# The modulation vectors of a two-block model on one Trainium2 core: where their 96 slabs of weights are multiplied, and by which engine

## The chip, the cores and the metric

The program runs on one core of a Trainium2 chip. The metric is device time in microseconds (us) from start to end of one execution, the lower the better; the time stated for a kernel is the median of several executions.

The engines are called TensorE (PE in the profile, with PEld for its weight loads), VectorE (DVE), ScalarE (ACT), GpSimd (POOL) and SyncE (SP, which here only starts transfers). Each runs its own list of instructions in order, and waits on semaphores for the others.

## The reference, cut to what matters

The model is one block (delta rule, dilated attention, expert layer) and then two layers of a second block, over 512 latent tokens and 256 context tokens of width 1024. The change touches only the six modulation vectors of each layer of the second block:

```
s_lat = jax.nn.silu(c)
s_ctx = jax.nn.silu(c_ctx)
for i in range(DEPTH_2):
    mod = (s_lat @ w_mod[i] + b_mod[i])[:, None, :]
    mod_c = s_ctx @ w_mod[i] + b_mod[i]
    sh1, sc1, g1, sh2, sc2, g2 = jnp.split(mod, 6, axis=-1)
    ...
    h = rms_norm(x, norm_mix[i]) * (1.0 + sc1) + sh1
    ...
    x = x + g1 * y
    h = rms_norm(x, norm_ffn[i]) * (1.0 + sc2) + sh2
    x = x + g2 * swiglu(h, w_gate[i], w_up[i], w_down[i])
```

`w_mod[i]` is 1024 x 6144 in fp32. Two vectors (latent and context) are multiplied with it, so there are 6144 x 2 results a layer: much to load (24 MB a layer) and little to compute. Nothing in it depends on the tokens, so it may be done at any time before its first use.

## The kernel before

**Slabs.** All weights come as slabs of 128 x 1024 fp32 (512 KB), in one list called `spine`, through four buffers `raw0` to `raw3` that `load_sync` fills in the order of the list. Slab i may be loaded when slab i-4 is done with its buffer.

**Units.** A slab of an ordinary weight is a *unit*: ScalarE rounds it to `whi` (L524), VectorE subtracts to get `wlo` (L532), each into one of three buffers, and TensorE does 24 matmuls: 16 with `whi` (L600, L602) and then 8 with `wlo` (L611). The buffer `raw` is free when `wlo` is made.

**Modulation.** `w_mod` is 96 slabs: six groups (l, r), l the layer and r the third of its 6144 columns, of 8 row blocks k times 2 halves. In `mod_tensor` a slab is two fp32 matmuls with a stationary operand of 32 columns (`svec`, the two input vectors) and 512 columns of the slab streamed; half 0 uses columns 0 to 63 of the array, and half 1 columns 64 to 127. The halves of one k stand next to each other in the list and run as one *pair* of slabs, four column groups side by side, in one PSUM bank a group. When a group's 16 slabs are done, `mod_end` copies the bank to SBUF on ScalarE, transposes it on TensorE (L932) and adds the bias on VectorE (L942, L949).

**Order.** Everything is laid out before the kernel is built by a planner (`Weave`): it keeps a clock for each engine, with costs for each kind of instruction, and each side stream (an attention lane, a chain) places its next step when its inputs are expected. `split_ahead` places the splits of up to two units ahead of the one that runs. `drain` runs side streams alone, when no unit may go on. The stages, by the trace's time: the convolutions' units (to about 100 us), delta rule and dilated attention beside projections `u_da` (to 527), four units of the merge and `u_z` (to 588), 20 units of the merge and `u_out` (to 764), the context's two layers and the experts, and then each latent layer: its mixer's units and local ("near") attention, output projection, feed-forward network (`net0`, `net1`).

**Where the slabs stand before.** `coupled(main, halves)` spreads pairs over a list of units: 8 pairs beside the convolutions, 8 beside the last 12 units of `u_da`, 16 beside 26 units of the merge and `u_out`, 1 + 13 beside `net0`, and 2 at the start of the second latent layer. (The first pairs of these last two stand just ahead of the first units of their stage.) In the near attentions there is nothing of them: `lat` calls `drain` for the four lanes, of which each item does scores, softmax, eight transposes (L2562), and the product with the values (L2571), on pairs of PSUM banks listed in `near_lane`.

## Time and profile before

| | |
|---|---|
| time, three runs | 3846.35, 3853.12, 3858.47 us; median 3853.12 |
| span of the profiled execution | 3848.4 us (it has no other time of its own) |
| TensorE busy | 3718.6 us, 97% of the span |
| VectorE busy | 2396.7 us, 62% |
| ScalarE busy | 1577.5 us, 41% |
| GpSimd busy | 840.9 us, 22% |
| memory traffic | 647 MB, 168 GB/s over the span |

### The profile page before, as it was taken

What the parts mean: (1) busy time and instruction counts of PE and PEld (TensorE: products, weight loads), DVE (VectorE), ACT (ScalarE), POOL (GpSimd) and SP (SyncE); (2) the same over time, 40 slices, a digit from 0 to 9 for tenths busy, and PEclk for the clock granted to TensorE, in tenths of its full rate; (3) what the DMA queues carried; (4) which work ended last, traced back from release to release, by engine and by line L of the source; (5) the groups of instructions that cost most, each with busy time, mean ns of one, the idle gap of its engine ahead of it and who ended that gap; (6) DMA issues with size and microseconds to landing.
All of it is one profiled execution on the core that took longest, in us unless ns stands there. A gap on an engine that the chain in (4) does not pass through costs nothing.

```text
span 3848.4 us, 56344 instructions
## 1 busy us (share of the span) xinstructions
PE 3718.6 (97%) x22665; PEld 3215.4 (84%) x22665; DVE 2396.7 (62%) x4154; ACT 1577.5 (41%) x2538; POOL 840.9 (22%) x695
## 2 busy tenths in 40 slices
PE   8999999989999999999999999998999999899998
PEld 5788777788899899999999999777777777677887
DVE  6455433466899668888888887567533345764333
ACT  4523343444335653333333335446422243653222
POOL 0112000153116454344344343010100010100000
PEclk9999999999999999999999999999999999899999
DMA  5211245533355679999999995320333432112332
GB/s 206 82 47 45 91 141 184 194 108 100 96 175 190 221 253 358 345 330 346 325 345 332 346 333 184 94 76 28 111 121 126 137 131 69 58 39 88 99 95 75
DMA packets 213908, 647.03 MB, mean 168 GB/s; under 512 B 19760, under 2 KB 65840, under 8 KB 210064
## 3 DMA queue, kind: packets, MB, share of 16 engines
q1 hardware_dynamic: 162816, 459.47, 35.8%
q0 software_dynamic: 50832, 183.95, 13.1%
q8 instruction: 180, 2.95, 0.3%
q14 instruction: 80, 0.66, 0.1%
HBM read 615.13 MB, written 27.79 MB: 167 GB/s over the span
## 4 chain that ended last, share of the span: by engine, by line
PE 86%; DVE 8%; ACT 4%; issue 1%; DMA 1%; POOL 0%; SPq 0%; DVEq 0%; ACTq 0%
PE ps L600 22%; PE ps L611 22%; PE ps L602 21%; PE ps L557 4%; PE ps L3502 2%; PE ps L2544 1%; PE ps L2571 1%; PE ps L2562 1%; PE ps L909 1%; DVE hlo_plain L774 1%; ACT l_NS L2594 1%; PE ps L2147 1%; PE ps L1240 1%; PE ps L1575 1%; PE ps L1231 1%
## 5 line engine op out<-in xcount | busy, mean ns | idle before, releaser
L600 PE MATMUL ps<-hhi,whi 128*128 128x512 f32 (+1 forms) x2824 | 1060.5, 376 | 3.6 <-DVE xres L3089 2.9
L532 DVE TENSOR_TENSOR wlo<-raw,whi 128x1024 fp32r<-128x1024 f32 x543 | 666.6, 1228 | 598.7 <-ACT whi L524 588.9
L602 PE MATMUL ps<-hlo,whi 128*128 128x512 f32 (+1 forms) x2824 | 1033.1, 366 | 0.2
L524 ACT ACTIVATE whi<-raw 128x1024 fp32r<-128x1024 f32 x616 | 648.5, 1054 | 596.9 <-PE ps L611 410.2
L611 PE MATMUL ps<-hhi,wlo 128*128 128x512 f32 (+1 forms) x2824 | 653.7, 370 | 0.0
L600 PEld LDWEIGHTS ps<-hhi,whi 128*128 128x128 f32 x2824 | 532.7, 189 | 104.1 <-issue 23.5
L602 PEld LDWEIGHTS ps<-hlo,whi 128*128 128x128 f32 x2824 | 531.7, 188 | 68.8 <-issue 4.1
L611 PEld LDWEIGHTS ps<-hhi,wlo 128*128 128x128 f32 x2824 | 499.8, 188 | 73.8 <-issue 6.8
L600 PE MATMUL ps<-ag_hi,whi 128*128 128x352 f32 x1024 | 328.6, 324 | 0.0
L602 PE MATMUL ps<-ag_lo,whi 128*128 128x352 f32 x1024 | 327.6, 321 | 0.0
L532 POOL TENSOR_TENSOR wlo<-raw,whi 128x1024 fp32r<-128x1024 f32 x74 | 183.8, 2492 | 161.0 <-ACT whi L524 158.8
L3751 POOL DMA_INDIRECT fetched<-peer_v_rows,rows x128 | 152.1, 1188 | 224.9 <-DVE xtok L3700 206.0
L3751 POOL DMA_INDIRECT fetched<-peer_u_rows,rows x128 | 152.0, 1188 | 215.4 <-DVE ract L3680 203.5
L602 PEld LDWEIGHTS ps<-ag_lo,whi 128*128 128x128 f32 x1024 | 192.5, 188 | 0.0
L600 PEld LDWEIGHTS ps<-ag_hi,whi 128*128 128x128 f32 x1024 | 192.1, 188 | 0.0
L3589 ACT ACTIVATE uact<-ps 128x352 f32<-128x352 f32 x128 | 59.6, 465 | 322.9 <-PE ps L611 322.9
L685 POOL COPY nacc<-nsq 128x512 f32<-128x512 f32 x6 | 3.7, 611 | 845.9 <-ACT nsq L674 845.9
L611 PE MATMUL ps<-ag_hi,wlo 128*128 128x352 f32 x1024 | 186.1, 323 | 0.0
L611 PEld LDWEIGHTS ps<-ag_hi,wlo 128*128 128x128 f32 x1024 | 168.0, 188 | 0.0
L3700 DVE SCALAR_TENSOR_TENSOR xtok<-fetched,ract,xtok 128x1024 f32<-128x1024 f32 x127 | 162.5, 1279 | 0.0
L3680 DVE CUSTOM_DVE_ANT_0 fetched<-fetched,xtok 128x1024 f32<-128x1024 f32 x128 | 156.0, 1219 | 0.1
L600 PE MATMUL ps<-hchi,whi 128*128 128x256 f32 x512 | 134.2, 296 | 7.8 <-ACT c_gg L2002 3.1
(677 smaller groups left out, 6208.5 us busy)
## 6 DMA issues: line engine op xcount, KB each, us to landing
raw<-w_in SPq DMA_DIRECT2D x151, 512.0 KB, 3.8
raw<-peer_u SPq DMA_DIRECT2D x128, 512.0 KB, 6.6
raw<-peer_v SPq DMA_DIRECT2D x128, 512.0 KB, 6.2
raw<-w_mod SPq DMA_DIRECT2D x96, 512.0 KB, 4.1
raw<-w_gate SPq DMA_DIRECT2D x66, 512.0 KB, 3.6
raw<-w_up SPq DMA_DIRECT2D x66, 512.0 KB, 3.6
raw<-w_down SPq DMA_DIRECT2D x66, 512.0 KB, 3.6
gate_dram<-stage SPq DMA_DIRECT2D x22, 1024.0 KB, 4.7
```

Of the source, the lines that this page charges most:

```text
L524: a.x.activation(whi[n % NW][:], raw[i % NRAW][:], ACT.Copy, bias=0.0, scale=1.0).then_inc(*a.gives("hi", i))
L532: e.x.tensor_tensor(wlo[n % NW][:], raw[i % NRAW][:], whi[n % NW][:].bitcast(F32), ALU.subtract).then_inc(*e.gives(*lo_sig(i)))
L557: ins = t.x.matmul(o, w[:, 128 * (first + k):128 * (first + k) + 128], p.plain, start=grp.opens and k == 0, stop=grp.closes and k == len(g ...
L600: t.x.matmul(o, w, p.hi, start=grp.opens and k == 0, stop=False)
L602: t.x.matmul(o, w, p.lo, start=False, stop=False)
L611: ins = t.x.matmul(o, lo[:, 128 * (starts[gi] + k):128 * (starts[gi] + k) + 128], p.hi, start=False, stop=grp.closes and k == len(grp.pair ...
L774: v.x.scalar_tensor_tensor(p.plain, self.nm.x[c], self.gain(c), self.nm.r[:], ALU.mult, ALU.mult).then_inc(*v.gives("apply_v", self.name, ...
L3502: ins = t.x.matmul(four(b, x), ea[n % 4][:, x, :], eb[n % 4][:, x, :], start=True, stop=True)
L3589: a.x.activation(uact[j % 2][:], held(("out", "peer_u", j))[:, 0:TD], ACT.Gelu_apprx_tanh, bias=0.0, scale=1.0).then_inc(*a.gives("peer_a" ...
L3680: v.x.tensor_tensor_reduce(c[:], c[:], xtok[:], 1.0, 0.0, ALU.mult, ALU.add, ract[:, i:i + 1]).then_inc(*v.gives("expert_v", "dot", i))
L3700: v.x.scalar_tensor_tensor(xtok[:], c[:], ract[:, i:i + 1], xtok[:], ALU.mult, ALU.add).then_inc(*v.gives("expert_v", "sum", i))
L3751: g.x.indirect_dma_start(fetched[i % NF][:], None, io["peer_v_rows" if i >= NU else "peer_u_rows"], bass.IndirectOffsetOnAxis(ap=at_, axis ...
```

## The change

The 96 slabs are laid out again, each group with its first half's eight slabs ahead of the second half's, so that neighbours share the same half of the array's columns. Three things replace the pairs:

- group (0,0), 16 slabs: single or two after one another by TensorE beside the convolutions' units (`between`);
- groups (0,1), (0,2), (1,0), 48 slabs: VectorE multiplies each slab with its two scalars a partition and adds it up in two SBUF buffers (`mod_vector`, L935 for the first slab of a half and L938 for the others, two instructions of 128 x 1024 a slab). After each half TensorE sums over the partitions with four fp32 matmuls (`mod_sum`, L958);
- groups (1,1) and (1,2), 32 slabs: TensorE again, inside the `drain` of the near attention of the first and of the second latent layer. There `fill` (`mods_beside`) places a slab whenever the planner sees TensorE free until 0.6 us before the next step. What is left is placed at the end of the drain, and `modend` is drained too. The two upper near lanes lose the bank pair (0, 1), which the modulation takes.

```diff
-    def drain(self, *names, until=None):
+    def drain(self, *names, until=None, fill=None):
...
+            if fill and fill(at[n] - 0.6):
+                self.flush()
+                continue
...
-def coupled(main, halves):
-
-    out, n, blocks = [], 0, len(halves) // 2
+def between(main, other):
+    out, n = [], 0
     for i, u in enumerate(main):
-        upto = -(-blocks * (i + 1) // len(main))
-        out += halves[2 * n:2 * upto] + [u]
+        upto = min(len(other) * (i + 1) // (len(main) - 1), len(other))
+        out += [u] + other[n:upto]
         n = upto
     return out
...
-            y.wait_ge(*(("mod_t", i - NRAW) if before.kind == "mod" else end(i - NRAW) if before.direct else lo_sig(i - NRAW)))
+            y.wait_ge(*(mod_done(i - NRAW) if before.kind == "mod" else end(i - NRAW) if before.direct else lo_sig(i - NRAW)))
...
+    def mod_vector(v, i):
+        l, r, half, k = spine[i].key
+        if (l, r) not in mod_acc:
+            return
+        v.wait_ge(f"raw{i % NRAW}", i)
+        v.wait_ge("svec_a")
...
+        for w in range(2):
+            acc, col = mod_acc[l, r][w], svec[:, 2 * k + w:2 * k + w + 1]
+            if k == 0:
+                ins = v.x.tensor_scalar(acc[:], raw[i % NRAW][:], col, None, ALU.mult)
+            else:
+                v.wait_ge("modacc_v", l, r, half, k - 1, w)
+                ins = v.x.scalar_tensor_tensor(acc[:], raw[i % NRAW][:], col, acc[:], ALU.mult, ALU.add)
+            ins.then_inc(*v.gives("modacc_v", l, r, half, k, w))
...
+            t.wait_ge("sel_g", 1)
+            t.wait_ge("modacc_v", l, r, half, KC - 1, n - 1)
+            for w in range(n):
+                for x in range(2):
+                    j = 2 * half + x
+                    ins = t.x.matmul(b[32 * j:32 * j + 32, :], sel[:, 1 - w:33 - w], mod_acc[l, r][w][:, 512 * x:512 * x + 512],
+                                     start=w == 0, stop=w == n - 1, tile_position=(0, 32 * j))
...
-             [(6, 7), (2, 3), (0, 1), (4, 5)]),
+             [(6, 7), (2, 3), (4, 5)]),
...
-    spine += u_dn[:2] + coupled(u_dn[2:], m0[:16]) + u_da[:-12] + coupled(u_da[-12:], m0[16:32]) + u_merge[:4] + u_z
-    spine += coupled(u_merge[4:] + u_out[:6], m0[32:] + m1[:16]) + u_out[6:]
+    spine += u_dn[:2] + between(u_dn[2:], m0[:16]) + u_da[:-12] + between(u_da[-12:], m0[16:32]) + u_merge[:4] + u_z
+    spine += between(u_merge[4:] + u_out[:6], m0[32:] + m1[:16]) + u_out[6:]
...
-    spine += lm0.units + u_lout[0] + net0.units[:2] + m1[16:18] + coupled(net0.units[2:], m1[18:44])
-    spine += lm1.units[:2] + m1[44:] + lm1.units[2:] + u_lout[1] + net1.units
+    spine += lm0.units + u_lout[0][:2] + m1[16:32] + u_lout[0][2:] + net0.units
+    spine += lm1.units + u_lout[1][:2] + m1[32:] + u_lout[1][2:] + net1.units
...
+        def fill(until):
+            if not left:
+                return False
+            split_to(left[0] - 1)
+            if left[0] >= at_unit["loaded"]:
+                return False
+            here_at = plan.expected([(f"raw{left[0] % NRAW}", (left[0],))])
+            if max(here_at, plan.now()) > until:
+                return False
+            plan.clock["tensor"] = max(plan.now(), here_at)
+            mod_piece(left.pop(0))
+            return True
...
-        plan.drain(*[lane.name for lane in near], *[f"split {m.name} {i}" for i in range(3)], f"gla {m.name}")
+        fill = mods_beside(l + 1)
+        plan.drain(*[lane.name for lane in near], *[f"split {m.name} {i}" for i in range(3)], f"gla {m.name}", fill=fill)
+        while fill(1e8):
+            pass
+        plan.drain(f"modend1{l + 1}")
```

How instructions move shows at three places. The first is TensorE beside the convolutions; `raw`,`svec` rows are slabs of the modulation, `whi` and `wlo` rows are units. Before:

```order
38 L637 MATMUL ps<-hlo,whi_67 128x512 x8
39 L909 MATMUL ps<-raw_64,svec 32x512 x2
40 L909 MATMUL ps<-raw_65,svec 32x512 x2
41 L600 MATMUL ps<-hhi,whi_68 128x512
42 L602 MATMUL ps<-hlo,whi_68 128x512
```

After the change:

```order
73 L613 MATMUL ps<-hhi,wlo_70 128x512 x8
74 L918 MATMUL ps<-raw_64,svec 32x512 x2
75 L918 MATMUL ps<-raw_65,svec 32x512 x2
76 L602 MATMUL ps<-hhi,whi_68 128x512
77 L604 MATMUL ps<-hlo,whi_68 128x512
```

The rows look alike, but the two slabs of a place were two halves of one k and are now two k of one half. There were 8 such places; there are now 6 with two slabs and 4 with one.

The second place is VectorE beside the first merge unit whose results it takes (`gate` rows are the merge's evacuation, `mg_lo` the lower part of its result). Before:

```order
419 L532 TENSOR_TENSOR wlo_70<-raw_64,whi_67 128x1024
420 L532 TENSOR_TENSOR wlo_71<-raw_65,whi_68 128x1024
421 L532 TENSOR_TENSOR wlo_69<-raw_64,whi_66 128x1024
422 L1812 TENSOR_TENSOR gate_first_154<-ps,gate_first_154 128x512
423 L1813 TENSOR_TENSOR gate_first_155<-ps,gate_first_155 128x512
424 L1815 TENSOR_TENSOR gate_first_154<-gate_first_154,gate_first_155 128x512
425 L1818 TENSOR_TENSOR mg_lo<-gate_first_154,mg_hi 128x512
```

After the change:

```order
458 L534 TENSOR_TENSOR wlo_70<-raw_66,whi_67 128x1024
459 L1863 TENSOR_TENSOR gate_first_161<-ps,gate_first_161 128x512
460 L1864 TENSOR_TENSOR gate_first_162<-ps,gate_first_162 128x512
461 L1866 TENSOR_TENSOR gate_first_161<-gate_first_161,gate_first_162 128x512
462 L938 SCALAR_TENSOR_TENSOR macc_98<-raw_65,svec,macc_98 128x1024
463 L938 SCALAR_TENSOR_TENSOR macc_99<-raw_65,svec,macc_99 128x1024
464 L1869 TENSOR_TENSOR mg_lo<-gate_first_161,mg_hi 128x512
465 L938 SCALAR_TENSOR_TENSOR macc_98<-raw_63,svec,macc_98 128x1024
466 L938 SCALAR_TENSOR_TENSOR macc_99<-raw_63,svec,macc_99 128x1024
467 L938 SCALAR_TENSOR_TENSOR macc_98<-raw_64,svec,macc_98 128x1024
468 L938 SCALAR_TENSOR_TENSOR macc_99<-raw_64,svec,macc_99 128x1024
469 L534 TENSOR_TENSOR wlo_71<-raw_65,whi_68 128x1024
```

Two or three slabs' instructions now stand between one unit's `wlo` and the next.

The third place is TensorE in the near attention of the first latent layer, which has no unit at that time. Before:

```order
8734 L2571 MATMUL ps<-l_NS_467,l_nvtok 64x128
8735 L2562 MATMUL ps<-cst,l_NS_478 128x128 x8
8736 L2562 MATMUL ps<-cst,l_NS_445 128x128 x8
8737 L2562 MATMUL ps<-cst,l_NS_456 128x128 x8
8738 L2544 MATMUL ps<-l_nks_396,l_nqd_394 128x256
```

After the change:

```order
8694 L2595 MATMUL ps<-l_nks_399,l_nqd_397 128x256
8695 L2613 MATMUL ps<-cst,l_NS_474 128x128 x8
8696 L918 MATMUL ps<-raw_65,svec 32x512 x2
8697 L918 MATMUL ps<-raw_66,svec 32x512 x2
8698 L918 MATMUL ps<-raw_63,svec 32x512 x2
8699 L918 MATMUL ps<-raw_64,svec 32x512 x2
8700 L918 MATMUL ps<-raw_65,svec 32x512 x2
8701 L2613 MATMUL ps<-cst,l_NS_485 128x128 x8
8702 L2622 MATMUL ps<-l_NS_474,l_nvtok 64x128
```

The 16 slabs of a layer stand at nine places of its near attention, one to five at each; this is the longest run.

## Rows read from the trace of the kernel before

**Rows 1.** The page: busy time, slices of the span, chain by engine.

```profile
PE 3718.6 (97%) x22665; PEld 3215.4 (84%) x22665; DVE 2396.7 (62%) x4154; ACT 1577.5 (41%) x2538; POOL 840.9 (22%) x695
...
PE   8999999989999999999999999998999999899998
...
PE 86%; DVE 8%; ACT 4%; issue 1%; DMA 1%; POOL 0%; SPq 0%; DVEq 0%; ACTq 0%
```

**Rows 2.** Windows of `u_da` with slabs, merge with slabs, two near attentions (columns named).

```profile
core 0: us, PE busy (x) PEld busy (x) DVE busy (x) ACT busy (x) POOL busy (x), PEclk, DMA share, GB/s
434.90:527.00 92.10, 90.91 (x479) 67.20 (x480) 33.73 (x56) 35.31 (x54) 2.19 (x4) 1.00 0.52 183
588.10:753.50 165.40, 163.75 (x768) 120.47 (x768) 64.46 (x87) 55.21 (x78) 15.92 (x19) 1.00 0.58 207
2570.60:2635.50 64.90, 49.12 (x375) 39.30 (x373) 45.30 (x119) 42.37 (x87) 7.59 (x11) 0.78 0.17 53
3299.00:3367.00 68.00, 51.53 (x388) 41.37 (x387) 47.58 (x123) 45.70 (x93) 9.55 (x13) 0.81 0.17 50
```

**Rows 3.** Timeline of PE beside the convolutions: start, length, line, operation.

```profile
40.10 1.07 PE L909 MATMUL ps<-raw,svec 128*32 128x512 f32 x8
...
46.77 1.06 PE L909 MATMUL ps<-raw,svec 128*32 128x512 f32 x8
47.76 0.50 PE L600 MATMUL ps<-hhi,whi 128*128 128x512 f32 x1
...
53.33 0.39 PE L600 MATMUL ps<-hhi,whi 128*128 128x512 f32 x1
...
59.86 0.50 PE L600 MATMUL ps<-hhi,whi 128*128 128x512 f32 x1
```

**Rows 4.** Timeline of PE, ahead of the latent layers' first units.

```profile
2738.26 1.92 PE L909 MATMUL ps<-raw,svec 128*32 128x512 f32 x16
2742.59 0.47 PE L630 MATMUL ps<-hhi,whi 128*128 128x512 f32 x1 [2.41 <-ACT hhi L741]
...
3121.34 1.92 PE L909 MATMUL ps<-raw,svec 128*32 128x512 f32 x16
3125.68 0.47 PE L630 MATMUL ps<-hhi,whi 128*128 128x512 f32 x1 [2.41 <-ACT hhi L741]
```

**Rows 5.** Timeline of PE at a norm's sum: one fp32 matmul of 512 columns.

```profile
764.34 1.02 PE L694 MATMUL ps<-nacc,ones 128*128 128x512 f32 x2
765.20 1.88 PE L697 MATMUL ps<-nsq,ones 128*128 128x512 f32 x4
```

**Rows 6.** The page's costliest groups: busy us, mean ns, idle before.

```profile
L532 DVE TENSOR_TENSOR wlo<-raw,whi 128x1024 fp32r<-128x1024 f32 x543 | 666.6, 1228 | 598.7 <-ACT whi L524 588.9
...
L524 ACT ACTIVATE whi<-raw 128x1024 fp32r<-128x1024 f32 x616 | 648.5, 1054 | 596.9 <-PE ps L611 410.2
...
L3700 DVE SCALAR_TENSOR_TENSOR xtok<-fetched,ract,xtok 128x1024 f32<-128x1024 f32 x127 | 162.5, 1279 | 0.0
```

**Rows 7.** One line of DVE, an fp32 tensor-scalar instruction of 512 columns.

```profile
L1009 DVE TENSOR_SCALAR cacc<-cbuf,cst x12: 478/486/489, 28.7 to 99.3; 128x512 f32<-128x512 f32 x12
```

**Rows 8.** Waits of PE and DVE, 588.1 to 753.5 us: total, times, longest.

```profile
PE ps L600 <- ACT whi L524: 1.6, 2, 0.8
...
DVE wlo L532 <- ACT whi L524: 79.0, 21, 9.2
```

**Rows 9.** Issues of slabs in 588 to 754 us, median us to landing.

```profile
raw<-w_mod SPq DMA_DIRECT2D x29, 512.0 KB, 4.3
raw<-w_in SPq DMA_DIRECT2D x15, 512.0 KB, 5.4
```

**Rows 10.** Timeline of PE in the first near attention: longest gaps, warm and slow transposes.

```profile
2570.61 1.04 PE L2562 MATMUL ps<-cst,l_NS 128*128 128x128 f32 x8
...
2575.29 0.66 PE L2562 MATMUL ps<-cst,l_NS 128*128 128x128 f32 x4 [2.78 <-DVE l_NS L2661]
...
2594.62 0.45 PE L2571 MATMUL ps<-l_NS,l_nvtok 128*64 128x128 f32 x1 [4.31 <-DVE l_NS L2667]
...
2628.86 0.45 PE L2571 MATMUL ps<-l_NS,l_nvtok 128*64 128x128 f32 x1 [3.40 <-DVE l_NS L2667]
...
2630.76 1.97 PE L2562 MATMUL ps<-cst,l_NS 128*128 128x128 f32 x8
```

More of the change, by code:

```diff
@@ L848, in first_gpsimd @@
         g.x.memset(svec[:], 0.0).then_inc(*g.gives("svec_g"))
+        g.x.memset(sel[:], 0.0).then_inc(*g.gives("sel_g", 0))
+        g.wait_ge("sel_g", 0)
+        g.x.memset(sel[:, 1:2], 1.0).then_inc(*g.gives("sel_g", 1))
     def first_scalar(a):
@@ L926, in tensor @@
         def tensor(t):
+            if (l, r) in mod_acc:
+                yield from mod_sum(l, r, 1)["tensor"](t)
             yield 0.3
@@ L955, in mod_ready @@
         return ("mod_v", l, 2, "gain", 1)
-    mods = [[Unit("mod", (l, r, k, h), io["w_mod"][((3 * l + r) * 8 + k) * 2 + h], T, [], None)
-             for r in range(3) for k in range(KC) for h in range(2)] for l in range(2)]
+    mods = [[Unit("mod", (l, r, h, k), io["w_mod"][((3 * l + r) * 2 + h) * 8 + k], T, [], None)
+             for r in range(3) for h in range(2) for k in range(KC)] for l in range(2)]
     evac = {}
@@ L1676, in z_scalar @@
             a.wait_ge("z_v", "gated", h)
+            a.wait_ge("modsum_t", 0, 1, 1)
             a.x.activation(odn_hi[:, h], zs[:, h], ACT.Copy, bias=0.0, scale=1.0).then_inc(*a.gives("z_a", "hi", h))
@@ L2758, in scalar @@
             idle(a)
+            if m.lat and out == 3:
+                a.wait_ge("modend_t", 1, m.l + 1)
             a.x.activation(hi, o, ACT.Copy, bias=0.0, scale=1.0).then_inc(*a.gives("split_a", m.name, out))
@@ L3864, in program @@
     lm1.idle, lm1.idle_load = [], [last_of("fdown", (net0, 1, HALF - 1))]
[L3865 removed]
+    lm1.idle_res = [("apply_v", "l1mix", "made", KC - 1)]
     for m in (cm0, lm0, lm1):
@@ L3948, in perform @@
         elif kind == "mod":
-            if e.name == "tensor":
+            if e.name == "vector":
+                mod_vector(e, what)
+            elif e.name == "tensor":
                 mod_tensor(e, what)
@@ L4011, in mod_piece @@
         raw_done(i)
-        l, r, k, half = spine[i].key
-        if k == KC - 1 and half == 1:
-            free = {(0, 1): [("chain0_v", "out", 3), ("chain1_v", "out", 3)], (0, 2): [("da_v", "oda", 3, 3)], (1, 0): [last_of("merge", KC - 1)]}.get((l, r), [])
+        l, r, half, k = spine[i].key
+        if k == KC - 1 and half == 0 and (l, r) in mod_acc:
+            plan.start(f"modsum{l}{r}", mod_sum(l, r, 0))
+        elif k == KC - 1 and half == 1:
+            free = {(0, 1): [("chain0_v", "out", 3), ("chain1_v", "out", 3)], (0, 2): [("da_v", "oda", 3, 3)], (1, 0): [last_of("merge", KC - 1)],
+                    (1, 1): [last_of("proj", (lm0, "sv", 0))], (1, 2): [last_of("proj", (lm1, "sv", 0))]}.get((l, r), [])
             plan.start(f"modend{l}{r}", mod_end(l, r, free))
@@ L4075, in pair, with mods_beside @@
             plan.pump()
+    def mods_beside(r):
+        left = [i for i, u in enumerate(spine) if u.kind == "mod" and u.key[0:2] == (1, r)]
+        mod_at[1, r] = rings["spine"][(turn["spine"] + 2) % 2]
+        def fill(until):
[10 more added lines that the diff above has]
+            return True
+        return fill
     def summed(use):
```

38 lines of the change are left out of this document (26 added, 12 removed).

## The prediction

> **What bounds the kernel now.** I read the page first: TensorE is busy for 97% of the span, in nearly every slice, and 86% of the chain that ended last is its own [rows 1]. So a microsecond of matmuls taken off a full stretch is a microsecond gained, until another engine falls behind. Then the windows of the stages that the change touches [rows 2]. Beside `u_da` TensorE is busy for 90.9 of 92.1 us with VectorE at 33.7, beside the merge for 163.8 of 165.4 us with VectorE at 64.5. The near attentions are different: 49.1 of 64.9 us and 51.5 of 68.0, that is 15.8 and 16.5 us idle, and a granted clock of only 0.78 and 0.81. The timeline there shows gaps of 2.8 to 4.3 us behind VectorE's softmax and copies, and the same eight transposes at 1.04 us warm and 1.97 us later on [rows 10].
>
> **What a pair of slabs costs now.** From the start of one pair to the next with one unit between is 46.77 - 40.10 = 6.67 us; two units and one pair take 59.86 - 47.76 = 12.10 [rows 3]. So a unit is 5.43 and a pair 1.24; I use 1.2. Of it 0.99 is from the pair's start to the next unit's (46.77 to 47.76), and the other 0.2 is lost in going in and out. Beside units all 48 pairs would be 58 us.
>
> **Convolutions.** Removed: 8 pairs, 9.6 us. Added: 16 slabs on two column groups each, at 10 places, 4 with one slab and 6 with two. Slabs of one half need the same columns, so two of them follow one another. No row shows two groups alone: four side by side take 0.99, and one fp32 matmul of 512 columns over the full width takes 765.20 - 764.34 = 0.86 from start to start [rows 3, 5]. I take 0.93, the middle, and 0.2 a place: 4 x 1.13 + 6 x 2.06 = 16.9 us, so **+7.3**. Bounds: 16 x 0.86 + 2.0 = 15.8 (+6.2), and 16 x 1.2 (+9.6). VectorE and the loads keep their work here.
>
> The Trainium skill (TensorEngine Tiling (Array Packing), "When to Use Tiling") gives a stationary operand of at most 32 columns a fourfold column tiling; two groups at a time would use half of it, and each slab would cost as much as a pair does. The trace of before holds only fours. By that rule this stage would come out at +9.6, the upper bound that the rows give as well.
>
> **Beside `u_da`.** 8 pairs go (-9.6). Two sums over the partitions come, each four fp32 matmuls on two column groups, like two slabs in a row: 2 x 2.06 = 4.1. **-5.5**. **Beside the merge:** 16 pairs go (-19.2), four sums come (+8.2): **-11.0**.
>
> **Latent layers.** 16 pairs go. Four of them stand ahead of the first units, and right behind them TensorE waits 2.41 us for `hhi` both times [rows 4]: their 2 x 1.9 us were hidden, and the waits will only be longer. The other 12 stand between units that run back to back: 12 x 1.2 = **-14.4**.
>
> These four terms are 7.3 - 5.5 - 11.0 - 14.4 = **-23.6 us**. Two costs stand against them.
>
> **VectorE as a bound.** 48 slabs are 96 instructions of 128 x 1024. Scalar-tensor-tensor in fp32 takes 1.279 us at that size [rows 6]; the tensor-scalar form takes 0.486 for 512 columns [rows 7], so about 0.91 for 1024 (twice, less a fixed 0.06). `u_da`: 28 x 1.28 + 4 x 0.91 = 39.5 us; merge: 56 x 1.28 + 8 x 0.91 = 79.0. VectorE is then at 33.7 + 39.5 = 73.2 of 92.1 - 5.5 = 86.6 us (85%) and at 64.5 + 79.0 = 143.5 of 165.4 - 11.0 = 154.4 us (93%). What hides it is that `wlo` is wanted two thirds into a unit and is split up to two units ahead; before, VectorE stood idle 79 us in this stage waiting for `whi` [rows 8]. That slack is spent. Queued behind two slabs' instructions (5.1 us, about a unit) are the next `wlo`, the merge's evacuation, and the release of the slab's buffer, for which the load of the slab after the next three waits. Such a load lands after 4.3 to 5.4 us [rows 9], a unit's then needs 1.05 us of ScalarE for `whi` [rows 6], some 6.5 us in all. The three slabs between give VectorE 7 us on average (143.5 us over 26 units and 32 slabs is 2.5 each), but only 3 x 1.23 = 3.7 where they are units. So some bubbles form on VectorE, and at 93% there is little room for them. The floor is none, when the lookahead evens all out. The nearest row for a late load is TensorE's wait for `whi` of 0.8 us, which happens twice in this stage now. If it comes at every third of the 26 units it is 7 us, at each 21. I take 5 us beside the merge and 1.5 beside `u_da`: **+6.5**, bounds 0 and 21. The dilated attention's steps stay as early in TensorE's order as before at their end, so I expect nothing from them.
>
> **The near attentions.** 32 slabs at 9 places in each layer: 32 x 0.93 + 18 x 0.2 = 33.4 us, against 32.3 us idle [rows 2]. So they do not fit into the gaps as they are. But a granted clock of 0.78 means that 2 x (1 - 0.78) = 44% of the time was at the lower level, 1.2 GHz; if the busy time is spread alike, 0.44 x 49.1 = 21.6 us of it ran at half speed and would be 10.8 us shorter at full. With slabs in the gaps I expect most of this back. TensorE then needs 38.3 + 16.7 = 55.0 of 64.9 us. Not all gaps are where the planner thinks, the slabs are not divisible, a load may be late, and the upper lanes choose among three bank pairs in place of four. I take 2 us a layer: **+4**. Bounds: 5 us a layer shorter than before (half of the 10.8 is on the lanes' chains), and the slabs' whole price. `modend` stands ahead of the lanes' last products in TensorE's order, and costs nothing at the end.
>
> The Trainium skill (TensorE: Matmul & The Clock Gate, "HAM oscillation — how this bites in real kernels") says that waits between bursts of matmuls drop the clock and that work kept running holds it up. The trace agrees: 0.78 with gaps of up to 4.3 us, 1.00 beside the merge. By that rule the slabs pay for a part of themselves, which is the rival "warm" below.
>
> Moved transfers: the same 96 slabs are loaded, only later by the same queue, into gaps of the network in the near attentions (a DMA share of 0.17 there [rows 2]). GpSimd gets two small fills at the start. Neither has a price.
>
> **Sum:** -23.6 + 6.5 + 4 = **-13.1 us**. Against the profiled span, 3848.4 - 13.1 = 3835.3. The median of the runs shown lies 4.7 us above that span, so I predict 3853.1 - 13.1 = **3840 us**. A measurement of this kernel can tell about 0.3%, 11.6 us, from no change.
>
> **The rivals.**
>
> *Warm near attentions.* The slabs hold TensorE at 2.4 GHz, and transposes and products on the lanes' chains go from 1.97 to 1.04. For it: the slow rows stand behind the gaps. Against it: VectorE is busy for 45.3 and ScalarE for 42.4 of the 64.9 us, and they wait for one another more than for TensorE. With 5 us less a layer and VectorE's waits at 3: -23.6 + 3 - 10 = -30.6, 3822 us. Chance 0.22.
>
> *Partly given back.* VectorE's waits at 14 us, or the attentions at 6 us a layer more: -23.6 + 14 + 4 = -5.6, 3847 us, up to the measuring limit on the other side. Chance 0.15, all of it within 0.3%.
>
> *VectorE takes over beside the merge (slower).* One mechanism: the release of `raw` by VectorE. Each load waits for VectorE's turn, `whi` for the load, `wlo` for both, and VectorE stands idle for it at each unit. For it: 93%, and the 3.7 us against 6.5. Against it: the average of 7 us, and the split two units ahead. If TensorE waits w at each of 26 units, the sum is -23.6 + 1.5 + 4 + 26 w: zero at w = 0.7, slower by 0.3% from w = 1.14, and at w = 1.2 it is +13, 3866 us. Chance 0.07.
>
> *The slabs do not fit the near attentions (slower).* At their whole price, -23.6 + 6.5 + 33.4 = +16.3, 3869 us. It is slower by 0.3% from 14.4 us more a layer. For it: the gaps are the lanes' latency, and a slab placed wrongly delays a lane. Against it: nine places in planned gaps. Chance 0.06.
>
> **How the numbers follow.** The forecast has 0.50, with a range of its own from -22 to -5 us; about 0.30 of it is beyond -11.6. Faster: 0.30 + 0.22 = 0.52. Within 0.3%: 0.20 + 0.15 = 0.35. Slower: 0.13. For 8 in 10, the range runs from the middle of "warm" (-33 with the bounds of the convolutions) to the middle of the slower cases: 3820 to 3862.
>
> **What the profile after would show.** Beside the convolutions: rows of two records' pairs with 0.9 to 1.0 us a slab, the stage 7 us longer. Beside the merge: a window 6 us shorter, VectorE at 90% or more, and waits of TensorE for `wlo` or `whi` that sum to 5 us; over 20 would prove the first slower rival. In the feed-forward networks: no slabs, units at 5.4 us back to back, 2.4 us waits for `hhi` of over 4 us. In the near attentions: a clock above 0.9, a length within 3 us of 64.9 and 68.0. The prediction is wrong if the clock stays at 0.8 there and the stages grow by 10 us each, or if they become shorter than 60.

## The result, and the profile after

The changed kernel takes 3886.98 us (median of 5 runs, 3883.79 to 3889.64), before took 3853.12; the ratio is 1.0089, 95% interval 1.0078 to 1.01. It is slower by 0.9%, where 0.34% faster was forecast and the range ended at 3862. The profiled execution took 3883.79 us with a span of 3882.0.

From the page of the changed kernel: busy time and count of each engine, slices, chain by engine [rows 1].

```profile
PE 3728.9 (96%) x22521; PEld 3221.9 (83%) x22521; DVE 2508.9 (65%) x4250; ACT 1579.4 (41%) x2538; POOL 851.2 (22%) x697
...
PE   8999999889999999999999999999899999989998
...
PE 84%; DVE 9%; ACT 4%; issue 2%; DMA 1%; POOL 0%; DVEq 0%; SPq 0%; ACTq 0%
```

It hardly shows where the time went: four slices of TensorE fell from 9 to 8 and two rose, and VectorE has 112 us more work. So I set both traces side by side by units: unit n begins with the first matmul of its weight slab (from 460 on the bounds lie up to 1.8 us beside it, by the same in every kernel), slabs of the modulation are not counted, and the same unit does the same work in every kernel here. Times between unit starts, in us, from the traces' instruction starts (0 to 37: convolutions and the first of `u_da`; 37 to 57: the rest of `u_da`, dilated attention, gates; 57 to 75 and 75 to 85: nearly all of the 26 units of merge and output that have slabs; 460 to 480 and 569 to 577 hold the near attentions, 480 to 545 the first latent network; a pair of 1.2 us may fall on the other side of a bound):

```
              0-37   37-57   57-75   75-85   85-460  460-480  480-545  545-569  569-577  577-598
before       419.75  152.87  112.75   64.59  1675.10  275.79   377.65   183.39   169.16   123.78
after        426.81  158.39  122.06   81.02  1673.35  279.33   362.92   185.03   177.29   122.81
```

The differences are +7.1, +5.5, +9.3, +16.4, -1.7, +3.5, -14.7, +1.6, +8.1 and -1.0: +34.1 us. Forecast were +7.3, -4 (with 1.5 of waits), -6 for both stretches of the merge together (with 5), 0, and for the latents -14.4 + 4. The network is right to half a microsecond, the convolutions to about one (their stretch also lost one pair of `u_da`, 1.2 us). The merge is off by 31.7 us, `u_da` by 9.5, the near attentions by 7.6.

Windows of the two stretches from unit 57 to 75 and 75 to 85, with the columns of [rows 2]. First before:

```profile
589.20:701.90 112.70, 111.97 (x528) 82.45 (x525) 37.03 (x45) 31.27 (x38) 4.23 (x8) 1.00 0.59 212
701.90:766.50 64.60, 63.67 (x289) 47.71 (x288) 34.23 (x49) 28.56 (x46) 18.52 (x15) 1.00 0.53 180
```

and after:

```profile
601.70:723.80 122.10, 108.06 (x454) 84.75 (x452) 81.82 (x86) 31.28 (x39) 4.73 (x8) 0.96 0.54 181
723.80:804.80 81.00, 69.81 (x273) 51.97 (x273) 63.87 (x72) 28.48 (x46) 21.81 (x15) 0.92 0.49 158
```

TensorE was idle for 1.7 us of 177.3; now it is for 25.2 of 203.1, and its granted clock has gone from 1.00 to 0.96 and 0.92: part of its matmuls ran at 1.2 GHz. By the forecast the stage had 11.0 us less to do and should have taken 166.3. It took 36.8 more, of which 23.6 are idle time and 13.2 busy time. Some 11 of these are the same matmuls at the lower clock (an estimate from the two rows: 0.04 of 122.1 us and 0.08 of 81.0). (One of the 16 pairs stood just ahead of unit 57; counted there, 35.6 are over.) VectorE is busy for 145.7 us, near the forecast of 143.5 for a window cut slightly otherwise, but that is 72% of what the stage now takes, not 93%: it has idle time too, so something passes to and fro between the two. The waits say for whom TensorE stood, in this stage of the changed kernel:

```profile
ACT whi L526 <- DMA raw<-w_in: 20.8, 8, 3.7
...
PE ps L602 <- ACT whi L526: 19.9, 7, 4.0
...
ACT whi L526 <- DMA raw<-w_br: 14.4, 5, 5.3
...
PE ps L613 <- DVE wlo L534: 4.8, 2, 4.3
```

So of TensorE's 25.2 idle us, 19.9 are spent on `whi`, which is ScalarE's and which waits for the load, and only 4.8 on VectorE's `wlo`.

The DMA queue's own waits there, after:

```profile
SPq L518 <- DVE macc L938: 135.8, 28, 11.2
SPq L518 <- DVE macc L935: 23.4, 4, 14.0
```

Before, the queue waited 134.6 us there for TensorE's slab matmuls and 28.6 for `wlo`. As a share of the stage it waits no longer than before, about nine tenths; what changed is for whom. Now a load waits for VectorE's second instruction on the slab in whose buffer it lands. One instance, in the timelines of three engines and the queue (start, length, what; the idle time before it in brackets). VectorE:

```profile
666.27 1.22 DVE L534 TENSOR_TENSOR wlo<-raw,whi 128x1024 fp32r<-128x1024 f32 x1
667.40 0.69 DVE L1869 TENSOR_TENSOR mg_lo<-gate,mg_hi 128x512 fp32r<-128x512 f32 x1
668.00 7.26 DVE L938 SCALAR_TENSOR_TENSOR macc<-raw,svec,macc 128x1024 f32<-128x1024 f32 x6
675.45 1.23 DVE L534 TENSOR_TENSOR wlo<-raw,whi 128x1024 fp32r<-128x1024 f32 x1 [0.18 <-ACT whi L526]
```

SP's queue:

```profile
657.28 0.33 SPq L518 DMA_DIRECT2D raw<-w_mod  x1
658.42 0.33 SPq L518 DMA_DIRECT2D raw<-w_in  x1
666.38 0.80 SPq L518 DMA_DIRECT2D raw<-w_mod  x2
670.51 0.33 SPq L518 DMA_DIRECT2D raw<-w_br  x1
670.88 0.43 SPq L518 DMA_DIRECT2D raw<-w_mod  x1
672.90 0.33 SPq L518 DMA_DIRECT2D raw<-w_in  x1
675.29 0.33 SPq L518 DMA_DIRECT2D raw<-w_mod  x1
```

ScalarE:

```profile
674.28 1.06 ACT L526 ACTIVATE whi<-raw 128x1024 fp32r<-128x1024 f32 x1 [0.87 <-DMA raw<-w_br]
```

TensorE:

```profile
675.49 0.47 PE L602 MATMUL ps<-odn_hi,whi 128*128 128x512 f32 x1 [2.71 <-ACT whi L526]
```

Three slabs stand in a row on VectorE, 7.26 us. At 670.5 the first of them is added up and frees its buffer; only then is the merge unit's slab loaded. The slab issued right behind it, at 670.88, goes into a buffer that the `wlo` of 666.27 had freed before, but the loads keep the order of the list. The unit's slab lands about 3.8 us after its issue, ScalarE needs 1.06 us for `whi`, and TensorE, which had finished the unit before, stands still for 2.71 us until 675.49.

### The profile page after: what moved, and what is told of

It reads as the page before. It is cut to its first block, busy times and chain, and to the rows that moved or that the text cites. A ratio compares the mean times of both kernels' runs of the same rounds, so it can differ in the third digit from the quotient of the medians.

```text
span 3882.0 us, 56209 instructions
## 1 busy us (share of the span) xinstructions
PE 3728.9 (96%) x22521; PEld 3221.9 (83%) x22521; DVE 2508.9 (65%) x4250; ACT 1579.4 (41%) x2538; POOL 851.2 (22%) x697
## 4 chain that ended last, share of the span: by engine, by line
PE 84%; DVE 9%; ACT 4%; issue 2%; DMA 1%; POOL 0%; DVEq 0%; SPq 0%; ACTq 0%
PE ps L602 22%; PE ps L613 21%; PE ps L604 21%; PE ps L559 4%; PE ps L2595 2%; PE ps L3555 2%; PE ps L2622 1%; PE ps L2613 1%; DVE hlo_plain L776 1%; PE ps L918 1%; DVE macc L938 1%; ACT whi L526 1%; PE ps L2198 1%; PE ps L1290 1%; PE ps L632 1%
## 5 line engine op out<-in xcount | busy, mean ns | idle before, releaser
L602 PE MATMUL ps<-hhi,whi 128*128 128x512 f32 (+1 forms) x2824 | 1064.2, 377 | 18.6 <-ACT whi L526 14.8
```

What stands on the lines that cost most here:

```text
L602: t.x.matmul(o, w, p.hi, start=grp.opens and k == 0, stop=False)
```

## The experiments

There are two theories of the loss beside `u_da` and the merge. T1: the buffers; a slab added up by VectorE keeps one of the four for longer, so a unit's slab is loaded, split and multiplied late. T2: VectorE's queue; its added instructions stand ahead of the units' `wlo` and of the evacuations, whoever frees the buffers. The experiments' times by units, in the same stretches as above:

```
              0-37   37-57   57-75   75-85   85-460  460-480  480-545  545-569  569-577  577-598
e1           422.58  154.86  112.72   63.69  1676.18  283.44   362.91   185.07   177.25   122.83
e4           422.35  155.49  114.70   71.24  1674.45  283.36   363.52   185.39   176.06   123.59
e5           428.52  159.97  104.96   77.07  1673.31  284.09   363.18   185.31   175.26   123.76
e7           428.93  160.00  106.03   70.79  1678.15  283.70   363.19   185.31   178.21   124.03
e8           419.58  159.85  122.75   81.47  1675.48  284.02   363.02   185.13   177.27   122.83
e9           419.37  159.58  123.03   81.14  1675.04  283.95   363.13   185.19   175.91   123.06
b1           420.40  152.88  100.03   78.49  1676.96  286.63   362.92   185.07   175.24   123.80
e2           421.11  153.97  112.76   63.73  1672.97  280.60   363.21   185.32   175.16   123.86
e10          421.08  153.44  112.72   63.67  1680.48  283.63   363.12   185.25   175.14   123.88
e3           422.44  153.38  112.75   63.70  1673.34  282.70   362.24   182.80   172.68   124.06
v3           421.35  154.96  112.75   63.98  1674.68  276.47   363.21   185.34   171.79   123.87
b3           422.60  152.89  109.09   65.69  1677.25  280.05   362.21   182.79   175.25   122.85
```

The windows shown below are cut at the same bounds. e2 and e10 are one kernel, and so are e3 and v3, e8 and e9: profiled executions of the same code differ by steps of about 1.6 us, by 7.5 us in 85 to 460 and by 6.2 in 460 to 480. Only larger differences are read, or ones that repeat.

**e1: the latents' part alone.** The spine's rows put back, and the early vectors in pairs:

```diff
-    spine += u_dn[:2] + between(u_dn[2:], m0[:16]) + u_da[:-12] + between(u_da[-12:], m0[16:32]) + u_merge[:4] + u_z
-    spine += between(u_merge[4:] + u_out[:6], m0[32:] + m1[:16]) + u_out[6:]
+    spine += u_dn[:2] + coupled(u_dn[2:], m0[:16]) + u_da[:-12] + coupled(u_da[-12:], m0[16:32]) + u_merge[:4] + u_z
+    spine += coupled(u_merge[4:] + u_out[:6], m0[32:] + m1[:16]) + u_out[6:]
```

> Only the latents' part of the change: the 64 slabs beside the convolutions, u_da, the merge and u_out are put back on TensorE in pairs as before, the 32 of the latents stay single and between the near windows. Read unit by unit in the two traces, the change lost 38.2 us up to the end of the merge (gave 1.7 back in the context layer) and then, from the latents' start on, stood at +3.9 (layer 0's near attention), -15.2 (its network), +1.6 and +5.8 (layer 1 and its near attention), +2.4 and -0.9 (its network and the end). If the stages add up, this kernel stands at the sum of the latter alone, -2.4 us from before: about 3850.7, ratio 0.9994, inside what can be measured. If the latents' part was slowed by something that the early stages left behind, it comes out better, at the -13 to -14 that my prediction had for it alone (-14.4 with +4 of the near attentions: -10.4). Rival, that the latents' part is itself a loss: above 3858.

Measured 3854.77 us, ratio 0.9996 (0.9986 to 1.0005): no difference. The early stages take 112.7 and 63.7 us in 57 to 85, as before. The latents alone give 14.7 us in the network and lose 7.6 and 8.1 in the two stretches with near attentions. So the change's whole loss of 0.9% is made before the context layers, and its gain in the latents is eaten in the latents.

**e4: VectorE's work without the buffers.** On e1, VectorE does the 96 instructions on its accumulators alone:

```diff
-                ins = v.x.scalar_tensor_tensor(acc[:], raw[i % NRAW][:], col, acc[:], ALU.mult, ALU.add)
+                ins = v.x.scalar_tensor_tensor(acc[:], acc[:], col, acc[:], ALU.mult, ALU.add)
```

(The line taken out is the change's. Only the first instruction of each accumulator is the shorter tensor-scalar form here.)

> The kernel of e1, and VectorE does in the places of the 48 slabs the change's own two instructions each (the same shapes), but on its two accumulators alone: it reads no slab, frees no buffer, and nobody waits for it; TensorE does the slabs in pairs. Its extra results are not used. This tells the theories of the loss beside u_da and the merge (+4.6 and +24.6 us) apart. T2, VectorE's own time stands in front of the units' wlo in its queue: the stretch from the first slab beside u_da to the end of the merge is 20 to 35 us longer than in e1, about as the change against its expected gain (some 37 us apart). T1, the load chain (slab's buffer freed only by VectorE's second instruction, so the next w_in or w_br is loaded late, split late and multiplied late): here all buffers are freed as in e1, so it is within 5 us of e1.

From unit 57 to 85 it took 185.9 us against e1's 176.4: 9.5 more, between the two forecasts. In the windows of e4:

```profile
594.50:709.20 114.70, 112.57 (x528) 82.31 (x525) 90.32 (x93) 30.93 (x38) 4.79 (x8) 1.00 0.60 208
709.20:780.50 71.30, 66.28 (x290) 48.06 (x288) 58.41 (x65) 27.55 (x45) 21.98 (x15) 0.98 0.50 167
```

Beside the merge VectorE is busy for 90.3 of 114.7 us, more than in the change, and TensorE is idle for 2.1: a VectorE at 79% costs 2 us while it frees no slab's buffer. The other 7.6 us are beside the output units, where TensorE waits for ScalarE in small pieces of up to 1.9 us. Beside `u_da` (37 to 57) the work alone costs 0.6. T2 alone explains a quarter of the 36.8 us.

**e5 and e7: the change with more buffers.** VectorE's work stays, and so does the order of the list; loads take the buffer that has been idle longest, from six (e5) or five (e7), until the first (e5) or behind the sixth output unit (e7). The new ones lie at 175 and 201 KB, where that stage has room, and one `msb` moves for them:

```diff
-    raw = [sb(f"raw{i}", 9 + 4 * i, [1024]) for i in range(NRAW)]
+    raw = [sb(f"raw{i}", kb, [1024]) for i, kb in enumerate([9 + 4 * i for i in range(NRAW)] + [kb for kb, _ in EXTRA])]
...
+        ok = range(NRAW + (len(EXTRA) if m_from <= i < m_to else 0))
+        x = min(ok, key=lambda b: (last.get(b, -1), b))
```

> The change as it is, with two more buffers for loaded slabs (six in place of four) from the fourth slab of the merge's to the last unit before the first output unit. It leaves VectorE's work and order as in the change and takes away only that a load waits for a slab's last VectorE instruction. T1 (the load chain) expects the merge's stretch, units 57 to 85, to lose 12 to 20 of its +24.6 us, total 3865 to 3875. T2 (VectorE's queue in front of wlo) expects less than 5 of them, total above 3879.

3870.32 us in its one run. The first stretch, with six buffers, took 105.0 us for the change's 122.1, the second, with four again, 77.1 for 81.0. The windows of e5:

```profile
605.10:710.10 105.00, 103.30 (x454) 81.80 (x452) 81.27 (x87) 31.27 (x39) 4.73 (x8) 1.00 0.62 212
710.10:787.10 77.00, 67.30 (x271) 50.14 (x272) 66.86 (x72) 28.75 (x46) 22.01 (x15) 0.96 0.52 164
```

VectorE has the same 81 us of work in the first row as in the change, and TensorE is idle for 1.7 us in place of 14.0, at a clock of 1.00 in place of 0.96. The stretch is 7.8 us shorter than before, where eleven pairs gone and two sums added make 9.1: with the buffers, the change does there about what it was forecast to do.

> The change with one more buffer (five) from the fourth slab of the merge up to and with the sixth output unit; e5 had six, but four from the first output unit on. If the loads' buffers are the cause, the merge (units 57 to 75, +9.3 in the change and -7.8 in e5) stands between the two, and units 75 to 85 (+16.4 in the change, +12.5 in e5) lose at least 5 us. Rival: there it is VectorE's and ScalarE's chain of the norm that the added work delays (e4: +7.5 from unit 75 to 85 with no buffer concerned); then the fifth buffer takes off less than 5 of them.

3873.53 us. The windows of e7:

```profile
605.60:711.60 106.00, 103.55 (x453) 81.57 (x451) 81.17 (x86) 30.73 (x39) 4.72 (x8) 1.00 0.60 205
711.60:782.40 70.80, 65.40 (x272) 48.63 (x272) 62.34 (x67) 26.54 (x43) 21.45 (x15) 0.98 0.57 188
```

One buffer is enough for the merge (106.0), and kept through the output units it takes 10.2 us off them (70.8 for 81.0). One more buffer takes 26.3 of the 36.8 us away. The 10.5 left are close to the 9.5 that e4 found for VectorE's work alone.

The buffer isn't all that differs, though. The planner, which expects the loads earlier, lays the stage out anew: in e5 seven of its `wlo` stand elsewhere in VectorE's list than in the change, most of them some instructions earlier, ahead of slabs' work; in e7 more has moved. No run has more buffers with the change's order kept. What speaks for the buffers as the main cause is the changed kernel's own trace: its 19.9 us of waits for `whi` ended with a load and not with VectorE's list (in e7 they are 1.1), and waits for `wlo`, which the order can move, are 4.8 us in all.

**e8 and e9: the convolutions' slabs back in pairs**, in the change; e9 is the same kernel in five executions.

```diff
-    spine += u_dn[:2] + between(u_dn[2:], m0[:16]) + ...
+    spine += u_dn[:2] + coupled(u_dn[2:], m0[:16]) + ...
```

> The change with its first part alone undone: the 16 slabs beside the convolutions again in pairs, two halves of a group of rows together. The change stood 7.4 us behind before at the end of the convolutions (9.1 with a step of 1.6 at unit 23); predicted were 7.3. Expected: 7 to 9 us less than the change at unit 35, and the same less at the end, 3875 to 3877. Rival: the later stages wait for what doesn't depend on TensorE's pace (VectorE and the loads) and give part of it back: 4 us or less at the end.

> The kernel of e8 (the change with the convolutions' 16 slabs back in pairs), timed in rounds. Its one look stood 7.2 us ahead of the change at unit 35, 4.6 ahead at unit 85, and 2.4 behind it at the end, after steps of +1.6 (units 136 to 200), +1.6 and +3.1 (460 to 480, the latents' near attention), where both run the same code. If those steps are the spread of single executions (the change's profiled one was the fastest of its five, 3.2 us under their median), the convolutions' part costs 4 to 7 us at the end: ratio 1.0070 to 1.0079 against the change's 1.0089. Rival: what the convolutions lose is made up later by something that paces independently of it: ratio 1.0086 or more.

e8 took 3886.16 us in one run, e9 3884.21, ratio 1.0082 (1.0068 to 1.0095). Both miss what was expected of the total: 3875 to 3877 for e8, and e9 lies between the forecast's 1.0079 and the rival's 1.0086. By units e8's first stretch is 7.2 us shorter than in the change, as forecast, 37 to 85 longer by 2.6 and 85 to 480 by 6.8, in pieces that other kernels show too (e1, e4, e5 have the same 283 to 284 from 460 to 480 for the change's 279.3). Whether they are spread, or the lost time would have been made up there, the timings don't tell: their intervals hold both. What holds is the price in its own stretch; of it only 2.8 us show between the medians.

**e2, e3, e10, v3: the near attentions.** In both of them the changed kernel's first slab waits, here in layer 0:

```profile
2613.22 1.92 PE L918 MATMUL ps<-raw,svec 128*32 128x512 f32 x4 [4.97 <-ACT l_svT L2053]
```

for the evacuation of the newest unit from the bank that the modulation takes. e2, on e1, takes the other bank; e3 also has the two halves side by side, and the filler places pairs. e10 and v3 are e2 and e3 in eleven executions each.

```diff
-        mod_at[1, r] = rings["spine"][(turn["spine"] + 2) % 2]
+        mod_at[1, r] = rings["spine"][(turn["spine"] + 1) % 2]
...
             mod_piece(left.pop(0))
+            mod_piece(left.pop(0))
```

> The kernel of e1 with one number changed: the modulation's accumulator in the near attentions is the other bank of the two, whose last unit was evacuated earlier. In the change the first slab of each near attention waits 4.97 and 4.99 us for ScalarE's l_svT of the newest unit, which stands behind another evacuation that waits for VectorE. If that wait is TensorE's loss there (no window could have run meanwhile), each near attention is shorter by 3 to 5 us than in e1 and the total by 6 to 10. Rival: the wait fell into time in which nothing else could run, the lanes being still late; then the windows and slabs only trade places and less than 2 us in all is gained.

> The kernel of e2 (latents' slabs between the near windows, other bank), with these 32 slabs too in pairs: the two halves of one group of rows side by side, eight matmuls over four groups of PE columns in place of twice four over two, and the filler places a pair or nothing. In the change a single slab cost 0.92 to 1.0 us in the near attentions; a pair's cost there is the question. If a pair takes 1.2 us (as the page's mean of before has it), each near attention is shorter by 16 x 0.95 less 8 x 1.2 = 5.6 us where TensorE is what sets its pace, and the total 5 to 11 below e2's 3847. Rival: in the near attention the matmuls of slabs fill time that is there anyhow, or a pair finds room less often than a single slab: within 3 us of e2.

> The kernel of e2 (as e1, with the other bank for the modulation in the near attentions), timed in rounds. Between e1 (change's bank, single slabs: 0.9996) and e3 (other bank, pairs: 0.9976) it says how the 7.8 us go to the two edits. From the windows: the near attention of layer 0 took 67.4 us in e1, 64.7 in e2, 69.1 in b1 with e2's code at a lower clock, and 63.1 in e3; layer 1's 66.4, 66.7, 66.8, 62.9, and 1.7 us less in the gap behind it. So pairs are worth 3 to 4 us a layer, 6 to 7 of the 7.8, and the bank 0 to 2: expected ratio 0.9992. Rival: the bank takes the 4.9 us of waiting off each layer: ratio 0.9980 or less.

> The kernel of e3 once more, timed in rounds: all 64 slabs of the early stages in pairs on TensorE as before, the latents' 32 in pairs between the near windows with the other bank. Read by units it stood 4.7 us ahead of before at its end (e2, single slabs with the same bank, 2.1; e1, single slabs and the change's bank, 6.7 behind in a profiled execution that its ten timings put near before's own median). Single executions of before go from 3846 to 3860, so one look settles little. Expected: ratio 0.9975, interval below 1, a median near 3845. Rival: what one look of each showed was their spread, and it is within 0.3% of before.

e2's one run of 3847.35 us misled me: the median of the same kernel is 3856.91, ratio 1.0004 (0.9995 to 1.0013). The bank gives nothing. The wait of 4.97 us is gone, and the time stays: in e10's first near attention TensorE waits for the lanes and for a load instead.

```profile
PE ps L2623 <- DVE l_NS L2722: 3.8, 1, 3.8
PE ps L927 <- DMA raw<-w_mod: 3.2, 2, 2.7
PE ps L2605 <- DVE l_o L2732: 1.9, 1, 1.9
```

Pairs do give something: e3 took 3845.3 us, and v3, the same kernel, 3846.45, ratio 0.9976 (0.9967 to 0.9985), 10.5 us less than e10. The windows from the last latent unit ahead of the near attention to the next unit, of e10 and then of v3:

```profile
2578.40:2646.10 67.70, 58.09 (x445) 36.43 (x443) 44.78 (x119) 41.86 (x86) 7.59 (x11) 0.92 0.53 174
3302.80:3369.50 66.70, 57.09 (x444) 35.75 (x442) 44.51 (x121) 41.79 (x86) 7.60 (x11) 0.95 0.53 177
```

```profile
2574.80:2635.30 60.50, 51.39 (x444) 34.92 (x442) 43.94 (x119) 41.61 (x86) 7.59 (x11) 0.92 0.58 195
3292.10:3355.60 63.50, 53.40 (x445) 36.91 (x443) 44.21 (x121) 41.96 (x88) 7.59 (x11) 0.89 0.56 186
```

7.2 and 3.2 us shorter, with 6.7 and 3.7 us less for TensorE (e3's are 63.1 and 62.9). By units the mean of e3 and v3 is 2.5 us under that of e2 and e10 in 460 to 480, less than two executions of one kernel differ there, and 2.9 in 569 to 577, so the traces show about 5.5 of the 10.5 us between the medians; where the rest lies is open. That pairs make the kernel faster rests on the medians, whose intervals lie apart. Here a single slab, from e10's timeline:

```profile
2619.77 1.05 PE L927 MATMUL ps<-raw,svec 128*32 128x512 f32 x4
```

and a pair, from v3's:

```profile
2611.14 1.06 PE L927 MATMUL ps<-raw,svec 128*32 128x512 f32 x8
```

Twice the matmuls in the same time. e10's waits of 3.2 us for `w_mod` don't occur in v3. The first near attention with 8 pairs inside took 60.5 us, where before had 65.1 with none: the granted clock is 0.92 for before's 0.78, and the lanes' work is done sooner.

**b1 and b3: VectorE where it pays.** Only the merge's 16 slabs on VectorE, with six buffers, the next 16 in pairs on TensorE; b1 (on e2) has these 16 between the first six output units, b3 (on e3) spaces all 32 as the change does.

```diff
-    spine += coupled(u_merge[4:] + u_out[:6], m0[32:] + m1[:16]) + u_out[6:]
+    spine += between((u_merge[4:] + u_out[:6])[:13], m0[32:]) + coupled((u_merge[4:] + u_out[:6])[13:], m1[:16]) + u_out[6:]
```

(b1: `between(u_merge[4:], m0[32:]) + coupled(u_out[:6], m1[:16])`.)

> The kernel of e2, with only the 16 slabs of the merge added up by VectorE, six buffers for loads there, and the 16 of the next vector on TensorE in pairs beside the output units. With six buffers the change's merge, units 57 to 75, went from 15.9 to 8.1 us against before, 7.8 won, and lost 12.5 again in units 75 to 85, after the last output load had to make do with four. If the release of buffers is the cause of the loss, this kernel keeps most of the win and has none of the loss: 3 to 8 us below e2, 3840 to 3844. Rival (VectorE's queue itself, which with the added work alone cost 9 us from unit 57 to 90 in e4, most of it beside the output units): within 2 us of e2 or above it.

> The kernel of e3, with the merge's 16 slabs added up by VectorE over the first 13 of the 26 units, six buffers there, and the next 16 in pairs on TensorE over the other 13. It differs from b1 in the spacing: b1 won 12.7 us in units 57 to 75 and lost 13.9 in units 75 to 85, where its 16 slabs stood between six output units. If that was the crowd of loads (22 slabs in some 40 us), the spacing brings the win back: eight pairs of 1.2 us off TensorE, two groups of sums of 1.9 to 2.4 onto it, 5 us net, and 3 to 7 below e3 with all else equal. Rival: VectorE's two instructions per slab delay the splitting here too, with six buffers for it; then the pairs saved are given back, and it is within 3 us of e3 or above.

b1 took 3857.4 us in its one run, where 3840 to 3844 was expected. Eleven pairs left the stretch from 57 to 75 and one sum came, 11.1 us net; it became 12.7 us shorter than e2's. But in 75 to 85 it has eight pairs for e2's four, which is 4.8 us of matmuls, and the other sum, 2.1, and took 14.8 us longer: some eight us are left, which I put down to the crowd of slabs. It gives back all that VectorE had won. b3 took 3842.47 us, ratio 0.9964 (0.995 to 0.9977), the fastest kernel of the study, 0.36% under before. In 57 to 75 seven pairs are gone (8.4) and two sums of 2.06 come: 4.3 due, 3.7 measured against v3; in 75 to 85 it loses 1.7. Of the 4.0 us between its median and v3's the trace places 2.0 there, and the two intervals overlap. (The eighth pair is gone ahead of unit 57, where executions of one kernel differ by more than its 1.2 us.) So most of b3's lead over before is v3's, the pairs in the near attentions.

## Why the prediction was wrong

**What bounds the kernel**: right. What the stages lost adds up to the whole, 34.1 us by the stretches and 33.6 by the spans, so nothing made it up. Idle time of TensorE cost more than its length: beside the merge 13.2 us more of busy time came on top, most of it by the lower clock. Left open is why e9, with the convolutions' 7.2 us taken back, is only 2.8 faster.

**Convolutions, +7.3**: right. 7.2 between e8 and the change. Single slabs cost what was taken for them, from the changed kernel's timeline:

```profile
38.51 1.05 PE L918 MATMUL ps<-raw,svec 128*32 128x512 f32 x4
39.49 0.50 PE L602 MATMUL ps<-hhi,whi 128*128 128x512 f32 x1
...
45.16 1.91 PE L918 MATMUL ps<-raw,svec 128*32 128x512 f32 x8
47.00 0.50 PE L602 MATMUL ps<-hhi,whi 128*128 128x512 f32 x1
```

0.98 for one and 1.84 for two, where 0.93 each was the estimate, and 0.99 is what two halves side by side took before [rows 3]. The Trainium skill (TensorEngine Tiling (Array Packing), "When to Use Tiling") gives fourfold column tiling for 32 columns; that two groups at a time run at half its rate follows from it, and the trace agrees, 0.98 for four matmuls against 0.99 for eight. The stretch came out below the +9.6 of that reading since two slabs in a row go in and out only once.

**Latent networks, -14.4**: right, -14.7 in the first, and all kernels with this part show it.

**VectorE's waits beside the merge, +5 (of +6.5)**: this is the step that failed. The term was 5 us and measured 36.8, with VectorE's own work and the lower clock in it. Its mechanism stood in the prediction twice, as a term and as the rival "VectorE takes over beside the merge", whose row of numbers holds: 36.8 us over 26 units are w = 1.4 us a unit, past the 1.14 from which it makes the kernel slower. What was wrong is the argument against it. "The three slabs between give VectorE 7 us on average" took an average where slabs come in groups: VectorE has three in a row for 7.26 us, the buffer of the first comes free after 2.5 of these, and the load, `whi` and the unit follow one after the other, 5.0 us from issue to matmul. That first slab had been issued at 657.28 (SP's queue above) and held its buffer for 13 us; of the three slabs issued between it and the late unit's, only one was a unit (658.42), so TensorE had 5.4 us of work to bridge them. VectorE's time for three slabs was the wrong yardstick: what counts is how many of them feed TensorE. And the two floors of the sum were taken from a stage without the mechanism: waits for `whi` of 0.8 us, twice, showed that TensorE released buffers early, not that VectorE would. A second part was left out altogether: the granted clock was 0.96 and 0.92 with the waits, and 1.00 and 0.98 with a fifth buffer, and 13.2 of the 36.8 us are TensorE's busy time. What is shown (e4, e5, e7): a fifth buffer, with the order that the planner then chooses, is worth 26 us, VectorE's work by itself about 10, most of it beside the output units.

**Beside `u_da`, -5.5 + 1.5**: wrong by 9.5 us. The same waits stand there, in the changed kernel:

```profile
527.58 0.78 PE L602 MATMUL ps<-hhi,whi 128*128 128x512 f32 x1 [2.26 <-ACT whi L526]
```

TensorE waits 6.9 us for `whi` in that stretch, and its clock is 0.98. e4 shows that VectorE's work alone costs 0.6 us there. That the rest is the buffers is argued from the merge; more buffers were not tried in that stage.

**Near attentions, +4**: the two stretches with them grew by 11.6 in the change (3.5 + 8.1), by 16 in e1. Inside the attentions the forecast holds: from 65.1 and 64.8 us they went to 64.9 and 66.4, +1.4, and the clock rose from 0.78 and 0.81 to 0.95 and 0.92. The loss stands right behind them, where the forecast had nothing. The two output units that follow, before and after in layer 0:

```profile
2635.50:2650.30 14.80, 14.48 (x70) 10.80 (x69) 11.96 (x33) 11.00 (x27) 0.00 (x0) 0.91 0.13 37
```

```profile
2671.90:2690.80 18.90, 16.29 (x71) 11.92 (x70) 13.28 (x35) 12.07 (x29) 0.00 (x0) 0.82 0.08 29
```

In layer 1 it is 14.8 and 19.0: +8.3 in all. Eight matmuls into the first of these units TensorE waits for ScalarE's copies of the next attention's keys, 0.32 us before and now 2.61:

```profile
2639.12 0.36 PE L2544 MATMUL ps<-l_skd,l_sqs 128*128 128x256 f32 x1 [0.32 <-ACT l_rskd L3025]
```

```profile
2676.59 0.35 PE L2595 MATMUL ps<-l_skd,l_sqs 128*128 128x256 f32 x1 [2.61 <-ACT l_rskd L3078]
```

Before, those eight matmuls began at half speed and took 3.1 us; now they take 2.1, ScalarE isn't done sooner, and behind the wait the clock falls. The two units are as long in e1, e10 and v3 (18.8 to 18.9 us in layer 0). What more the attentions could have given is shown by e10 to v3: halves placed alone use half of the columns for the same time (5.5 us for both layers by the traces, 10.5 by the medians), and loads are waited for (1.4 and 1.1 us in the change). The rule of the Trainium skill that was weighed there (TensorE: Matmul & The Clock Gate, "HAM oscillation — how this bites in real kernels") holds inside them: filled gaps kept the clock up, and in v3 the first near attention, with its pairs, is 4.6 us shorter than before's without any.

**Chances.** The rival that came true had 0.07, and its own condition was written beside it. It was weighed against an average, and the case to price was the worst group of neighbours in the list.

## What to carry to other kernels

Work that reads a loaded buffer also holds it: before moving it to an idle engine, ask when that engine, in its own order, will free the buffer, and follow the chain load, conversion, first use in the worst grouping and not in the mean. A buffer more is the cheap test of that theory, since it leaves all engines' work as it is; where a planner lays out the order, keep that fixed too. And when a matrix product has only a few columns of weights, keep all column groups filled, in gaps too.

## What the runs showed that I had not expected

- Four matmuls over two groups of 32 columns take 0.92 to 0.98 us, eight over four groups 0.99: the second half of the columns is free.
- The fp32 tensor-scalar instruction on 128 x 1024 takes 0.748 us on VectorE, less than the 0.91 that the prediction worked out from 0.486 for 512 columns; the scalar-tensor-tensor form takes 1.279.
- Filling a gap can move the loss behind it: the two units behind each near attention take 4 us longer in every kernel with filled attentions.
- A wait of 4.97 us can be worth nothing: with it gone (e10) the time of the stretch stayed; TensorE waited for the lanes and a load instead.
- Profiled executions of the same code differ by up to 7.5 us in one stretch, in steps of 1.6 us and more. A single execution (e2, 3847.35, for a median of 3856.91) can be off by all of a small effect.
